# Value pages on every fourth partition, a group of one page from each of four blocks, and the weights' low parts on VectorE in the page steps

## The reference

```
proj = rmsnorm(x) @ w_in            # 1024 -> 5632: q, k, v, g_a, u, v_s, g_b, m_a, m_b
out  = x + (sig(m_a) * (attn * silu(g_a)) @ w_pa + sig(m_b) * (sgu * silu(g_b)) @ w_pb) @ w_o
```

## Time and profile before

| | us |
|---|---|
| median of 3 runs | 565.19 (561.32 to 569.01) |
| the profiled execution | 564.61 |
| its span, first to last instruction | 562.8 |
| mean granted TensorE clock | 0.978 |

### The profile page before, as it was taken

One profiled execution on the slowest core, in us unless ns is written; L12 is line 12 of the kernel. 1 busy time (PEld: TensorE's weight loads), 2 busy tenths in 40 slices (PEclk: granted clock), 3 DMA queues, 4 the chain that ended last, 5 costly groups with the idle time before them and its releaser, 6 DMA issues.

```text
span 562.8 us, 13854 instructions
## 1 busy us (share of the span) xinstructions
PE 521.1 (93%) x5624; PEld 474.5 (84%) x5624; DVE 305.9 (54%) x710; ACT 179.9 (32%) x389; POOL 121.4 (22%) x108
## 2 busy tenths in 40 slices
PE   8999999999999999999984899799957899999994
PEld 5999999999999999988984789799846799998763
DVE  6623223577755665667642648875412264694524
ACT  6522222243433433544431222221331132233313
POOL 2101211314132123123132143441451100000002
PEclk9999999999999999999998899899988999999998
DMA  8647443686598999994999989999999795351004
GB/s 247 177 151 195 146 128 103 197 221 186 173 261 197 267 273 210 275 270 123 275 237 289 257 211 265 230 262 272 238 255 226 186 259 192 120 190 38 1 9 149
DMA packets 73561, 112.00 MB, mean 199 GB/s; under 512 B 5501, under 2 KB 35338, under 8 KB 73498
## 3 DMA queue, kind: packets, MB, share of 16 engines
q1 hardware_dynamic: 72122, 107.51, 71.8%
q0 software_dynamic: 1232, 3.36, 2.0%
q10 hardware_dynamic: 144, 0.26, 0.1%
HBM read 106.57 MB, written 4.53 MB: 197 GB/s over the span
## 4 chain that ended last, share of the span: by engine, by line
PE 70%; DMA 17%; DVE 6%; SPq 2%; issue 2%; POOL 1%; ACT 1%; POOLq 0%; DVEq 0%; ACTq 0%
PE BK L576 33%; DMA KRAW<-in_cache_k 17%; PE BK L596 9%; PE BK L916 8%; PE BK L731 4%; PE BK L745 4%; PE BK L665 2%; DVE KT L1326 2%; PE BK L793 2%; PE BK L810 2%; PE BK L800 2%; SPq L504 1%; PE BK L846 1%; PE BK L773 1%; DVE XR L1238 1%
## 5 line engine op out<-in xcount | busy, mean ns | idle before, releaser
L576 PE MATMUL BK<-XH,WH 128*128 128x272 f32 x672 | 202.7, 302 | 0.0
L576 PE MATMUL BK<-XH,WL 128*128 128x272 f32 x672 | 194.3, 289 | 0.0
L576 PE MATMUL BK<-XL,WH 128*128 128x272 f32 x672 | 194.3, 289 | 0.0
L1326 DVE STREAM_TRANSPOSE KT<-KRAW 128x512 f32<-128x512 f32 x128 | 88.6, 701 | 90.4 <-DMA KRAW<-in_cache_k 90.1
L576 PEld LDWEIGHTS BK<-XH,WH 128*128 128x128 f32 x672 | 127.6, 190 | 10.9 <-issue 10.2
L576 PEld LDWEIGHTS BK<-XL,WH 128*128 128x128 f32 x672 | 127.5, 190 | 0.0
L576 PEld LDWEIGHTS BK<-XH,WL 128*128 128x128 f32 x672 | 127.2, 189 | 0.0
L1686 POOL TENSOR_TENSOR WL<-WRAW,WH 128x1024 fp32r<-128x1024 f32 x32 | 76.7, 2397 | 217.6 <-ACT WH L965 217.6
L731 PE MATMUL BK<-KT,QW 128*32 128x128 f32 x1024 | 37.2, 289 | 26.5 <-DVE KT L1326 26.5
L965 ACT ACTIVATE WH<-WRAW 128x1024 fp32r<-128x1024 f32 x52 | 54.9, 1056 | 16.6 <-PE BK L596 16.0
L731 PEld LDWEIGHTS BK<-KT,QW 128*32 128x32 f32 x1024 | 27.7, 115 | 32.4 <-DVE KT L1326 28.9
(11 more groups left out here) (207 smaller groups left out, 807.1 us busy)
## 6 DMA issues: line engine op xcount, KB each, us to landing
KRAW<-in_cache_k SPq DMA_DIRECT2D x128, 256.0 KB, 6.4
WRAW<-in_w_in SPq DMA_DIRECT2D x21, 1024.0 KB, 8.6
VRAW<-in_cache_v SPq DMA_DIRECT2D x56, 256.0 KB, 5.5
VQT<-in_cache_v SPq DMA_DIRECT2D x28, 256.0 KB, 6.3
VEX<-in_cache_v SPq DMA_DIRECT2D x24, 256.0 KB, 7.9
VGU<-in_cache_v SPq DMA_DIRECT2D x20, 256.0 KB, 5.4
WO<-in_w_o SPq DMA_DIRECT2D x4, 1024.0 KB, 7.0
XR<-in_x_prompt SPq DMA_DIRECT2D x4, 512.0 KB, 5.6
```

Source lines behind the costliest of these rows:

```text
L576: last = mm(BK[h][:, 0:HALF], w[:, n % 2, k, :], x[:, k, cols], start=(i == 0 and w is WH and x is XA), stop=(i == KC - 1 and w is WL))
L1326: dve.transpose(KT[:, i % KB, :], KRAW[:, i % KR, :]).then_inc(kt_ok, 1)
```

## The change

A group now has pages first_of(q), +2, +4 and +6: the first or the second page of each of four blocks, so that two groups make eight pages. Key page j of a group is transposed into KT with a step of four elements in its output (KT has the page as its innermost index), and a group's 128 score columns run over row and page, the page innermost. Value page j goes to the partitions j, j + 4, ..., j + 124. The sums over blocks are made for two groups at a time, in every eighth step, over 256 columns. The subtractions of tiles 14 to 45 move from GpSimd's list into VectorE's, into step 4m, after the page's transpose, silu's second half and the prompt's gate.

```diff
+def first_of(q):
+    return 8 * (q // 2) + q % 2
...
-        KT = sb("KT", [P, KB, DA])
+        KT = sb("KT", [P, KB // 4, 16, 32, 4])
...
                 if i % 4 == 0:
-                    sp.load(k_regs, PTB[0:1, i:i + 4])
+                    sp.load(k_regs, PTB[0:1, first_of(i // 4):first_of(i // 4) + 7:2])
...
-                sp.load(v_regs, PTB[0:1, 4 * q:4 * q + 4])
+                sp.load(v_regs, PTB[0:1, first_of(q):first_of(q) + 7:2])
...
-                    sp.dma_start(VP[place][32 * j:32 * j + 32], cache_v[0, bass.ds(page, 1)].rearrange("a (b t) h d -> (a t) b (h d)", b=4)
+                    sp.dma_start(VP[place][j:P:4], cache_v[0, bass.ds(page, 1)].rearrange("a (b t) h d -> (a t) b (h d)", b=4)
                                  ).then_inc(v_ld[place], 16)
...
-                at4 = 4 * (q % 2)
...
-                        last = mm(SCB[b % 2][32 * c:32 * c + 32, x * P:(x + 1) * P], QW[:, f, :], KT[:, at4:at4 + 4, 32 * f:32 * f + 32],
+                        last = mm(SCB[b % 2][32 * c:32 * c + 32, x * P:(x + 1) * P], QW[:, f, :], KT[:, q % 2, f].rearrange("p t j -> p (t j)"),
...
-                dve.transpose(KT[:, i % KB, :], KRAW[:, i % KR, :]).then_inc(kt_ok, 1)
+                dve.transpose(KT[:, i // 4 % 2, :, :, i % 4], KRAW[:, i % KR, :].rearrange("p (f d) -> p f d", f=16)).then_inc(kt_ok, 1)
...
-                b, x = q // 4, q % 4
+                b, x = q // 4, q % 4 // 2
...
-                sc = SCB[b % 2][:, x * P:(x + 1) * P].rearrange("p (n k) -> p n k", n=2)
-                summed = dve.tensor_reduce(R[:, 2 * x:2 * x + 2], sc, AX.X, ALU.add)
-                if x == 3:
+                sc = SCB[b % 2][:, 2 * x * P:(2 * x + 2) * P].rearrange("p (k n) -> p n k", n=4)
+                summed = dve.tensor_reduce(R[:, 4 * x:4 * x + 4], sc, AX.X, ALU.add)
+                if x == 1:
                     link(summed)
-                    last_page = SCB[b % 2][:, 4 * P - 32:4 * P]
+                    last_page = SCB[b % 2][:, 3 * P + 3:4 * P:4]
...
-                peak = dve.tensor_reduce(KP[:, 2 * x:2 * x + 2], sc, AX.X, ALU.max)
-                if x == 3:
+                peak = dve.tensor_reduce(KP[:, 4 * x:4 * x + 4], sc, AX.X, ALU.max)
+                if x == 1:
...
-                if t % 4 == 1 and 5 <= t < PAGES:
+                if t % 8 == 1 and 9 <= t < PAGES:
                     page_sums(t // 4 - 1)
...
                 if block_at(t - 5) is not None:
                     prompt_gate(block_at(t - 5))
+                if t % 4 == 0 and 4 <= t <= 128:
+                    split_lo(n + 1)
...
-            def split_lo(n):
-                pool.wait_ge(w_hi, n + 1)
-                if n == N_QKV + 2:
-                    pool.wait_ge(w_lo, n)
-                pool.tensor_tensor(WL[:, n % 2], WRAW[:, n // 2 % 2, :, n % 2 * P:(n % 2 + 1) * P], f32(WH[:, n % 2]), ALU.subtract).then_inc(w_lo, 1)
...
-                if t % 4 == 0:
-                    split_lo(N_QKV + t // 4 + 1)
```

More of the change, by code:

```diff
@@ L1209, in split_lo @@
                 dve.wait_ge(w_hi, n + 1)
-                if n == T_PB + 2:
-                    dve.wait_ge(w_lo, n)
                 if n >= T_WO:
@@ L1392, in choose @@
                 wait(dve, pt_pe, b)
-                dve.tensor_tensor(SC[:].rearrange("p (n k) -> p n k", n=8), SCB[b % 2][:].rearrange("p (n k) -> p n k", n=8),
-                                  bass.AP(sel.tensor, sel.offset, [list(sel.ap[0]), [1, 8], [0, 64]]), ALU.add).then_inc(eb_ok, 1)
+                dve.tensor_tensor(SC[:].rearrange("p (x k n) -> p x k n", x=2, n=4), SCB[b % 2][:].rearrange("p (x k n) -> p x k n", x=2, n=4),
+                                  bass.AP(sel.tensor, sel.offset, [list(sel.ap[0]), [4, 2], [0, 64], [1, 4]]), ALU.add).then_inc(eb_ok, 1)
             def sums_out(b):
```

## The result

The changed kernel takes 558.68 us (median of 20 runs, 556.06 to 563.31), the kernel before 568.29 in the same comparison (559.22 to 577.25). The ratio of their undisturbed runs alone is 0.9913, with a 95% interval from 0.9884 to 0.9943, which is nearer to 1 than the quotient of the two medians over all runs, 0.983. A second comparison, with six runs (e12), gave 0.9818 (0.9761 to 0.9876). So the change makes the kernel faster, by one or two per cent where 4.8% was forecast, and 558.7 us lies above the range of 526 to 556. The profiled execution took 560.12 us, its span is 558.3.

What follows compares the result with a forecast made beforehand. The prediction took PE to bound the first half of the page steps and late key loads the second. From 564.6 us it took 29 for faster value pages and added 2 for VectorE's subtractions: 538 us, range 526 to 556.

Steps and rivals of the forecast that it cites:

- Transposes with a step of four in the output: VectorE's 128 key-page transposes: writing every fourth element costs no extra over 0.701 us each, 90 us in all.
- The prediction's other end: Upper price for VectorE's strided transposes: a second pass over 512 elements, +0.5 us each, 64 us in all.
- What bounds the kernel: Page steps: PE decides the first half, late key loads the second, where 35 us of PE time are lost.
- Value pages at the key pages' price: DMA loads: a spread value page takes a key page's 0.68 us instead of 1.19.
- Rival B: Value-page loads: spreading gives half the gain, about 0.9 us a page, 544 us in all; chance 0.25.
- C: Value-page loads: spreading does nothing, as rows read 32 apart may cause the slowness; 564 us; chance 0.14.
- The sum of 27 us: Whole kernel: 29 us recovered from faster value pages, less 2 us charged for low parts on VectorE.
- The 6 us of PE idle left in the bursts: Second half of the page steps: two bursts of extra loads still leave PE idle 6 us together.
- Low parts on VectorE: 32 subtractions moved from GpSimd cost VectorE 39.2 us, mostly hidden in idle time; 2 us charged.
- Sums over pages: VectorE's sums in 16 pairs of 256 elements: 13.2 us instead of 17.2, no effect on PE's path.
- Rival D: Strided transposes make VectorE the bound: 3.2 us more a group, first half +30, about 590 us; chance 0.07.
- The signs: Profile marks of a right forecast, including value pages over 300 GB/s, PE's transpose wait under 8 us, transposes at 0.70 us.

Runs made afterwards that it cites:

- e12: The changed kernel itself, unedited, measured again on one chip beside two variants: 558.73 us, ratio to before 0.9818.
- e3: Kernel before, with value pages spread over every fourth partition and low parts of tiles 14 to 45 on VectorE, transposes contiguous: 545.07 us.
- the lower row of the table: Transposes with a step of four: 555.8 us with low parts on GpSimd, 558.7 on VectorE; 13 us more than contiguous transposes in either column.
- e2: Kernel before, with only value pages spread over every fourth partition and columns reordered in the mask add: 542.93 us, ratio 0.9538.
- e8: Kernel with spread value pages alone, but each page on every second partition of one half of the tile: 569.77 us.
- e11: Repeat, on one chip, of the kernel before with spread value pages and low parts on VectorE, transposes contiguous: 545.47 us, ratio 0.9568.
- e9: Kernel with spread value pages alone, early value loads at steps 113, 118 and 122 instead of 113, 115 and 117: 544.31 us.
- e6: Changed kernel, but transposes write with a step of two elements instead of four, PE reading runs of two: 551.40 us.

## Why the prediction was wrong

The step that failed is "Transposes with a step of four in the output": "I take no extra". The transposes took 0.407 us more each, and that is where 7 to 11 of the 13 us between the changed kernel and e3 come from. The row that the step leaned on, a copy of 32 elements with such a step (L1270), shows no price. It isn't only too short for it: 0.407 us for 512 elements is 0.8 ns each, so 32 would show 25 ns, and the row shows 2. A copy is not a transpose; why it doesn't pay is not shown. The prediction's other end, +0.5 us each, was near the truth.

The gap from 538 to 558.7 us adds up to about 20: 13 for the lower row of the table, 3 for the spread (29 forecast, 26 measured), and 4 because the sum started from one execution of 564.6 us, where the medians of before are 568 to 570.

Point by point, in the order of the prediction:

- **What bounds the kernel**: right. The key loads decided the second half: take the value pages' slowness away and nothing else (e2), and the time falls by 26 us; give it back by half the reach (e8), and it is all there again.
- **Value pages at the key pages' price**: right, 369 to 380 GB/s against 383. Rival B (half the gain) and C (nothing) are out as readings of the spread. C's own reason, rows read 32 apart, is the same before, in e2 and in e8, and of these only e2 has the fast pages.
- **The sum of 27 us**: of the 29 us for the spread 26.0 came, by the medians of e2's comparison (568.9 to 542.9); with the low parts it is 23.8 and 24.8 for the 27 (e3, e11). The profiled executions give less, 562.8 to 543.3 us of span, as the profiled one of before was among its faster ones. The 6 us of PE idle left in the bursts were too few: PE still waits 10.5 us in e2. Moving the bursts (e9) didn't lower that, so their place isn't the cause, or not alone. The chain of e2 from 261 to 440 us has 12.9% in key pages that land late and 5.9% in SP's issue of value loads before them; no run tells the two apart.
- **Low parts on VectorE**: "I charge 2 us" is what the runs show, 545.5 against 542.9 and 558.7 against 555.8, though each difference is within the spread of its runs. The wait for ScalarE's high part is 16.4 us from 100 to 448 us, where the wait for the scores had been 4.0 in all: it took the place of other idle time, not of that wait. The relief was smaller than the 3.6 us: the LayerNorm step fell from 1.596 to 1.010 us (to 0.744 in e3).
- **Sums over pages**: 16 x (0.420 + 0.375) = 12.7 us, worked out as 13.2. The step in PSUM's columns that they read costs nothing that shows.
- **Rival D**: its mechanism is what happened, its price was not. It had VectorE 3.2 us heavier a group, the first half 30 us longer, the second without gain, and 590 us. Measured: 4 x 0.407 + 1.24 = 2.9 us heavier, the first fourteen groups 8 us longer, the next seventeen 14 us shorter. One mistake there was "a third usable" of VectorE's idle time: from 100 to 260 us it fell from 56 us to 27, so about half was usable. Another was the threshold of +0.3 us a transpose. It doesn't follow from D's own sum, where a third of 3.6 us is 1.2 and the subtraction alone asks for 1.22; and 0.407 us lies above it, yet the kernel became faster. So D was given the right place, 0.07 of the chance and far too sharp an end, and nothing stood between it and the forecast: a price of 0.4 us that eats half of the gain was no case of its own.
- **The signs**: value pages over 300 GB/s, the DMA digits and VectorE's wait for key pages came. PE's wait (13.5 us for under 8), the clock (down to 0.93 for 1.00), the groups of the second half (10.7 us for 8.8 to 9.2) and the transposes (1.108 us for 0.70) did not.

## What to carry to other kernels

A layout that one engine likes must be made somewhere, and its price depends on the engine and on how many instructions make it: the reordering cost 52 us of VectorE in 128 transposes, 1.1 us a group of PE in the scores' read, and 3.2 us of VectorE in the mask adds (8.6 us in e2 for 5.4 before). Take a strided form's price from a row of the same operation and length, or count the unknown one at its upper end and see if its engine has the room. And spread a transfer's partitions over the whole height of the tile: 32 partitions of one quarter or one half moved at 221 and 227 GB/s, 32 of all 128 at 369 to 380.

## What the runs showed of the hardware

- VectorE's 32 x 32 transposes of 128 x 512 float32 write with a step of two elements at no cost (0.701 us), with four at 1.108, with eight at 1.157.
- PE read 128 float32 columns in runs of two at nearly the contiguous pace (291 ns an instruction in e6, 289 in runs of 32 before), and at half of it when each element stood alone 2 KB from the next (430 ns; some 2.2 us a group against 1.01).
- SP needs about 0.75 us to issue a load onto 32 partitions with a step, 0.47 onto 32 neighbours (3.00 and 1.87 us for four). In the chain of the changed kernel this issue stands for 2.4% of the span.
